# Latent attention between two MLPs: gains in the weights, one token split, a query norm moved into the exponent, a mask as contraction rows, half of the queries turned late

## What is computed

```python
ckr = rms_norm(h, kv_norm) @ w_dkv                    # 256 latents + 32 rotary columns
c_kv = rms_norm(ckr[..., :256], kv_lora_gain)
kv = (c_kv @ w_ukv).reshape(b, s, 16, 64 + 64)        # keys without position, values
k = rope_tail(rms_norm(concat(k_nope, k_rope), k_gain))
q = (rms_norm(rms_norm(h, b_attn_norm) @ w_dq, q_lora_gain) @ w_uq).reshape(b, s, 16, 96)
q = rope_tail(rms_norm(q, q_gain))
mask = key_chunk[None, :] <= (t // 64)[:, None]       # 64 tokens to a chunk
p = softmax(where(mask, q @ k * 96 ** -0.5, -1e30)); out = (p @ v) @ w_o
```

## Time and profile before

| | us |
|---|---|
| median of 3 runs | 1816.54 (1816.24 to 1817.72) |
| the profiled execution, whole | 1816.15 |
| its span in the profile | 1814.3 |
| TensorE busy | 1424.0 (78%) |
| VectorE, ScalarE, GpSimd busy | 550.1, 396.4, 144.9 |
| last matmul of the first MLP to first score of the latent attention | 1485.12 to 1567.00 |
| first score to output product | 1567.00 to 1600.46 |

### The profile page before, as it was taken

How to read it: one execution, slowest core, us unless ns; L and a number is a source line. 1 busy time by engine, 2 the same in 40 slices (tenths; PEclk the granted TensorE clock), 3 DMA queues, 4 the chain that set the end, 5 groups by cost and what they waited for, 6 DMA issues and landing times.

```text
span 1814.3 us, 20829 instructions
## 1 busy us (share of the span) xinstructions
PE 1424.0 (78%) x8548; PEld 856.4 (47%) x8548; DVE 550.1 (30%) x917; ACT 396.4 (22%) x587; POOL 144.9 (8%) x111
## 2 busy tenths in 40 slices
PE   4998978757675667667775767598899978799999
PEld 1884542212221122212221222176799967679997
DVE  1585340000000000000000000167455556635554
ACT  2413310000000000000000000156433344753331
POOL 2660000000000000000000000025200000420000
PEclk8998969787878787787877787789999998999999
DMA  9665539999999999999999999952255543224552
GB/s 378 246 181 223 243 154 422 427 428 428 429 428 429 429 428 428 428 429 429 428 429 428 428 428 429 414 190 89 93 186 186 185 154 99 93 93 143 189 190 105
DMA packets 79490, 542.80 MB, mean 299 GB/s; under 512 B 6370, under 2 KB 9579, under 8 KB 51538
## 3 DMA queue, kind: packets, MB, share of 16 engines
q1 hardware_dynamic: 75728, 535.99, 72.6%
q0 software_dynamic: 2000, 5.77, 1.4%
q10 hardware_dynamic: 1714, 0.36, 0.1%
HBM read 541.01 MB, written 1.08 MB: 299 GB/s over the span
## 4 chain that ended last, share of the span: by engine, by line
DMA 46%; PE 44%; DVE 5%; ACT 3%; issue 2%; POOL 0%; DVEq 0%; SPq 0%; ACTq 0%; POOLq 0%
DMA ring<-in_w_down 22%; DMA ring<-in_w_up 22%; PE bank L1189 10%; PE bank L1190 10%; PE bank L1191 10%; PE bank L1488 3%; PE bank L1505 3%; PE bank L1415 2%; DMA ring<-in_w_in 1%; PE bank L1219 1%; PE bank L1378 1%; PE bank L1359 1%; PE bank L1303 1%; ACT ring_parts L796 1%; DMA ring<-in_w_mod 1%
## 5 line engine op out<-in xcount | busy, mean ns | idle before, releaser
L1488 PE MATMUL bank<-ring,low 128*32 128x512 f32 x2016 | 324.7, 790 | 162.5 <-DMA ring<-in_w_up 137.1
L1488 PEld LDWEIGHTS bank<-ring,low 128*32 128x32 f32 x2016 | 67.7, 133 | 403.2 <-DMA ring<-in_w_up 211.7
L1505 PE MATMUL bank<-ring,low 128*32 128x512 f32 x1008 | 174.1, 828 | 96.0 <-DMA ring<-in_w_down 88.2
L796 ACT ACTIVATE ring_parts<-ring 128x4096 fp32r<-128x4096 f32 (+4 forms) x50 | 163.5, 3277 | 207.7 <-DMA ring<-in_mlp_w_down 94.9
L1781 DVE TENSOR_TENSOR ring_parts<-ring,ring_parts 128x4096 fp32r<-128x4096 f32 (+3 forms) x37 | 154.3, 4174 | 148.2 <-ACT ring_parts L796 148.2
L975 ACT ACTIVATE low<-bank 128x512 f32<-128x512 f32 x16 | 9.6, 597 | 855.8 <-PE bank L1488 855.8
L1189 PE MATMUL bank<-feat_parts,ring_parts 128*128 128x256 f32 x608 | 175.8, 289 | 12.6 <-DVE feat_parts L1845 10.4
L1190 PE MATMUL bank<-feat_parts,ring_parts 128*128 128x256 f32 x640 | 184.1, 288 | 0.0
L1191 PE MATMUL bank<-feat_parts,ring_parts 128*128 128x256 f32 x640 | 183.9, 287 | 0.0
L2107 DVE TENSOR_TENSOR low<-low,bank 128x512 f32<-128x512 f32 x16 | 11.0, 688 | 478.3 <-PE bank L1488 478.3
L1505 PEld LDWEIGHTS bank<-ring,low 128*32 128x32 f32 x1008 | 33.1, 132 | 220.9 <-DMA ring<-in_w_down 142.7
(11 more groups left out here) (345 smaller groups left out, 1968.4 us busy)
## 6 DMA issues: line engine op xcount, KB each, us to landing
ring<-in_w_gate SPq DMA_DIRECT2D x64, 2048.0 KB, 25.7
ring<-in_w_down SPq DMA_DIRECT2D x63, 2048.0 KB, 26.3
ring<-in_w_up SPq DMA_DIRECT2D x62, 2048.0 KB, 23.0
ring<-in_mlp_w_up SPq DMA_DIRECT2D x16, 2048.0 KB, 8.0
ring<-in_mlp_w_down SPq DMA_DIRECT2D x16, 2048.0 KB, 7.9
ring<-in_w_mod SPq DMA_DIRECT2D x12, 2048.0 KB, 11.8
ring<-in_w_in SPq DMA_DIRECT2D x4, 2048.0 KB, 19.1
ring<-in_a_w_in SPq DMA_DIRECT2D x3, 2048.0 KB, 20.1
```

What stands on the lines that cost most here:

```text
L796: last = act.activation(high(n, width)[:, cs], loaded(n, width)[:, cs], ACT.Copy)
L1488: last = pe.matmul((GATE if i < 4 else UP)[32 * j:32 * j + 32, :], xsT[:, k, :], held(n, 2)[:, kk, 512 * j:512 * j + 512], start=(k == 0), ...
L1505: last = pe.matmul(TURN[32 * g:32 * g + 32, :], hidT[:, c, 32 * j:32 * j + 32], held(n, 4)[:, c, 512 * d:512 * d + 512], start=(j == 0 and ...
```

## The change

- **Gains in the weights.** `weights_high` takes a gain and makes eight ScalarE instructions of a chunk, each with its own column of the gain as scale; `gained_low` on VectorE makes the low parts in eight. The inputs have one pair of parts, `hb`, without gain. The query-down split moves between the statistics of the two token tiles, and VectorE does three of its eight low pieces between the last residual and the norm of the second tile.
- **Order.** TensorE: `ckr` (each turned bank as it is ready), `dq` tile 0, turn of the key latents, `dq` tile 1, `ukv` tile 0, turn of the query latents, `ukv` tile 1, `uq`. The splits of the `uq` chunks stand behind the parts of the key latents. Key squares go to ScalarE and are summed by tile.
- **Query norm.** Queries are rotated and turned unscaled. The reciprocal root, one number for each query and head, multiplies the maximum on VectorE and is the scale of the exponential on ScalarE.
- **Mask.** Query and key rows grow from 96 to 98: two rows of ones and of -1e30, brought by two GpSimd DMAs from the constants into rows 96 and 97 of all 16 heads. VectorE's mask add goes. The keys now lie in `feat`, the queries in `low`.
- **Late turn.** The second half of the queries is rotated by VectorE in step 0 of the attention, and turned and copied out in step 1.
- **Output weights.** GpSimd makes both parts of both `wo3` chunks (`split_both`), after the mask transfers.

Context lines of the diff are left out too; the constants table (two rows of ones and -1e30 blocks at its end, the old mask removed), the numbering of splits and the statistics region are not shown.

```diff
...
-hkv, hb = parts(feat_r, 0, KD, T), parts(mid_r, 0, KD, T)
+hb = parts(feat_r, 0, KD, T)
...
+q_squares = [cut(v, 0, NT, HEADS // 2, QK_DIM) for v in (browf, xnf)]
+k_squares = cut(prob, 0, NT, HEADS, QK_NOPE)
+kT3, qT3 = cut(feat, 0, HEADS, T), cut(low, 0, HEADS, T)
+MASKED = QK_DIM + NT
...
-group("dq0", "dq1", chunk=dq_c)
-group("ckvT")
-group(*(f"ukv{t}{n}" for t in range(NT) for n in range(4)), chunk=ukv_c)
-group("dqT0", "dqT1")
+group("dq0", "ckvT")
+group("dq1", chunk=dq_c)
+group(*(f"ukv0{n}" for n in range(4)), "dqT0", "dqT1")
+group(*(f"ukv1{n}" for n in range(4)), chunk=ukv_c)
...
-group(*(f"k3T{i}" for i in range(8)), *(f"q3T{i}" for i in range(8)))
-pair_groups("la")
+group(*(f"k3T{i}" for i in range(4)), *(f"q3T{i}" for i in range(4)), *(f"k3T{i}" for i in range(4, 8)))
+LATE_TURN = 1
+pair_groups("la", {LATE_TURN: [f"q3T{i}" for i in range(4, 8)]})
...
-    pool.wait_ge(sem("q3"), 2)
-    split_low(wo3[0])
-    split_low(wo3[1])
+    def split_both(n):
+        width = width_of(n) // 8
+        full, count = loads(n)
+        pool.wait_ge(full, count)
+        pool.wait_ge(chunk_used, last_user(n, high_slot(n)))
+        for part in range(8):
+            cs = slice(width * part, width * (part + 1))
+            pool.tensor_copy(high(n, 8 * width)[:, cs], loaded(n, 8 * width)[:, cs]).then_inc(sem("w_high_pool"), 1)
+            pool.wait_ge(sem("w_high_pool"), 8 * wo3.index(n) + part + 1)
+            last = pool.tensor_tensor(low_part(n, 8 * width)[:, cs], loaded(n, 8 * width)[:, cs],
+                                      high(n, 8 * width)[:, cs].bitcast(F32), ALU.subtract)
+        last.then_inc(sem("w_low_pool"), 1)
+    for rows, at, after in ((kT3, C_MK, dq_c), (qT3, C_MQ, uq_c[1])):
+        pool.wait_ge(chunk_used, after + 1)
+        pool.dma_start(rows[QK_DIM:MASKED, :, :], I["constants"][0:NT, at:at + T].unsqueeze(1).to_broadcast([NT, HEADS, T]))\
+            .then_inc(sem("ld_mask"), 16)
+    split_both(wo3[0])
+    split_both(wo3[1])
...
-        last = act.activation(high(n, width)[:, cs], loaded(n, width)[:, cs], ACT.Copy)
+        if gain is None:
+            last = act.activation(high(n, width)[:, cs], loaded(n, width)[:, cs], ACT.Copy)
+        else:
+            for k in range(KD):
+                last = act.activation(split_as(n, KD, width // KD)[0][:, k, :], held_as(n, chunks[n])[:, k, :], ACT.Copy,
+                                      scale=vT[:, gain + k:gain + k + 1])
...
-    weights_high(dkv_c)
+    weights_high(dkv_c, gain=V_KV)
...
-    rms("rb", x, xn, D, lambda t: [(sem("xm0"), t + 1)])
-    weights_high(dq_c)
-    for name, dst, v in (("bT", hkv, V_KV), ("bTq", hb, V_B)):
-        for i in range(4):
-            act.wait_ge(*banks.filled(f"bT{i}"))
-            if name == "bTq":
-                act.wait_ge(sem("kv_lo"), i + 1)
-            for k in (2 * i, 2 * i + 1):
-                last = act.activation(dst[0][:, k, :], bk(f"bT{i}")[:, (k % 2) * T:(k % 2 + 1) * T], ACT.Copy,
-                                      scale=vT[:, v + k:v + k + 1])
-            last.then_inc(sem("hi_out"), 1)
+    rms("rb", x, xn, D, lambda t: [(sem("xm0"), t + 1)], [0])
+    weights_high(dq_c, gain=V_B)
+    rms("rb", x, xn, D, lambda t: [(sem("xm0"), t + 1)], [1])
+    parts_high("bT", hb)
...
+    q_junk = cut(prob, 512, NT, Q_LORA)
+    rms("rq", dq, q_junk, Q_LORA, lambda t: [drained(f"dq{t}")], [0])
+    latents_high("ckvT", ckvT, V_KVL, 0, 2)
...
-    latents_high("ckvT", ckvT, V_KVL, 0, 2)
-    rms("rq", dq, cut(prob, 512, NT, Q_LORA), Q_LORA, lambda t: [drained(f"dq{t}")])
+    rms("rq", dq, q_junk, Q_LORA, lambda t: [drained(f"dq{t}")], [1])
+    def key_squares(t):
+        for n in range(4):
+            act.wait_ge(*drained(f"ukv{t}{n}"))
+        act.activation(k_squares[:, t, :, :], kv[:, t, :, 0:QK_NOPE], ACT.Square).then_inc(sem("k_squares"), 1)
+    latents_high("dqT0", dqT, V_QL, 0, 2)
+    latents_high("dqT1", dqT, V_QL, 2, 1)
+    key_squares(0)
...
-    latents_high("dqT0", dqT, V_QL, 0, 2)
-    latents_high("dqT1", dqT, V_QL, 2, 1)
-    head_rms("k3", NT * HEADS, 1.0 / QK_DIM, 1)
-    for half in range(2):
-        if half:
-            act.wait_ge(sem("q3_ss"), half)
-        for t in range(NT):
+    key_squares(1)
+    def query_latents(half, tiles):
+        for t in tiles:
...
-                act.activation(q_squares[:, t, 4 * m:4 * m + 4, :], src, ACT.Square).then_inc(banks.drain_sem(g), 1)
-        head_rms("q3", HEADS, 1.0 / QK_DIM, half + 1)
-        weights_high(wo3[half])
+                act.activation(q_squares[half][:, t, 4 * m:4 * m + 4, :], src, ACT.Square)\
+                    .then_inc(banks.drain_sem(g), 1)
+    query_latents(0, [0])
+    head_rms("k3", NT * HEADS, 1.0 / QK_DIM, 1)
+    query_latents(0, [1])
+    query_latents(1, range(NT))
...
-    heads_out("q3T", qT3, V_QN, range(4))
-    attend_pairs("la", boT)
+    heads_out("k3T", kT3, V_KN, range(4))
+    act.wait_ge(sem("q3_ss"), 2)
+    act.activation(qs[1], qs[0], ACT.Sqrt, bias=eps, scale=1.0 / QK_DIM).then_inc(sem("q3_root"), 1)
+    heads_out("k3T", kT3, V_KN, range(4, 8))
+    def la_between(i):
+        if i == LATE_TURN:
+            heads_out("q3T", qT3, V_QN, (6, 7))
+    def la_scale(i, h):
+        n = HEADS * (i // 8) + head_at(i, h)
+        return qs[2][:, n:n + 1]
+    attend_pairs("la", boT, la_between, la_scale)
...
-    pe.wait_ge(sem("ckv_n"), 1)
-    turn_latents("ckvT", 0, 2, ckr)
-    pe.wait_ge(*drained("ckvT"))
-    need_split(ukv_c)
-    for t in range(NT):
+    def down_product(c, name, width, t, turned=None):
+        need_split(c)
+        token_major_split(f"{name}{t}", hb, split_as(c, KD, width), t * P, width, turned)
+    def keys_values(t):
...
+    down_product(dkv_c, "ckr", KV_LORA + QK_ROPE, 0, "bT")
+    down_product(dkv_c, "ckr", KV_LORA + QK_ROPE, 1)
+    down_product(dq_c, "dq", Q_LORA, 0)
+    pe.wait_ge(sem("ckv_n"), 1)
+    turn_latents("ckvT", 0, 2, ckr)
+    down_product(dq_c, "dq", Q_LORA, 1)
+    pe.wait_ge(*drained("ckvT"))
+    need_split(ukv_c)
+    keys_values(0)
...
+    keys_values(1)
...
+    turn_heads("k3T", K3, (sem("k3"), 1), range(4))
+    turn_heads("q3T", Q3, (sem("q3"), 1), range(4))
+    turn_heads("k3T", K3, (sem("k3"), 1), range(4, 8))
+    pe.wait_ge(sem("ld_mask"), 32)
+    def la_between(i):
+        if i == LATE_TURN:
+            turn_heads("q3T", Q3, (sem("q3"), 2), range(4, 8))
...
+        if t == 0:
+            pe.wait_ge(*drained(f"k3T{i}"))
+            pe.wait_ge(*drained(f"q3T{i}"))
...
-            last = pe.matmul(bk(f"laS{i}")[:, h * n:(h + 1) * n], qT3[0:QK_DIM, hh, t * P:(t + 1) * P],
-                             kT3[0:QK_DIM, hh, 0:n], start=True, stop=True)
+            last = pe.matmul(bk(f"laS{i}")[:, h * n:(h + 1) * n], qT3[0:MASKED, hh, t * P:(t + 1) * P],
+                             kT3[0:MASKED, hh, 0:n], start=True, stop=True)
...
-    pe.wait_ge(*drained("k3T7"))
-    pe.wait_ge(*drained("q3T3"))
-    pe.wait_ge(*drained("q3T7"))
-    attend_pairs("la", la_scores, la_values, bo, ident)
+    attend_pairs("la", la_scores, la_values, bo, ident, la_between)
...
-            add_biases(i, s)
-            dve.tensor_reduce(at_m[:, i % 4, :], s, AX, ALU.max, negate=True).then_inc(sem(pre + "_max"), 1)
+            if add_biases:
+                add_biases(i, s)
+            last = dve.tensor_reduce(at_m[:, i % 4, :], s, AX, ALU.max, negate=True)
+            if scales:
+                link(last)
+                last = dve.tensor_tensor(at_m[:, i % 4, :], at_m[:, i % 4, :], scales(i), ALU.mult)
+            last.then_inc(sem(pre + "_max"), 1)
...
+    def gained_low(n, gain, ks):
+        if ks[0] == 0:
+            dve.wait_ge(sem("w_high"), high_no(n) + 1)
+        w, hi, lo = held_as(n, chunks[n]), *split_as(n, KD, width_of(n) // KD)
+        for k in ks:
+            last = dve.scalar_tensor_tensor(out=lo[:, k, :], in0=w[:, k, :], scalar=vT[:, gain + k:gain + k + 1],
+                                            in1=hi[:, k, :].bitcast(F32), op0=ALU.mult, op1=ALU.subtract)
+        if ks[-1] == KD - 1:
+            last.then_inc(sem("w_low"), 1)
...
+                if t == 1:
+                    gained_low(dq_c, V_B, range(0, 3))
...
-    weights_low(dq_c)
-    for name, dst, v in (("bT", hkv, V_KV), ("bTq", hb, V_B)):
-        for i in range(4):
-            dve.wait_ge(*hi_out(f"{name}{i}"))
-            for k in (2 * i, 2 * i + 1):
-                last = lo_part(dst, k, bk(f"bT{i}")[:, (k % 2) * T:(k % 2 + 1) * T], v)
-            last.then_inc(sem("kv_lo") if name == "bT" else banks.drain_sem(f"bT{i}"), 1)
+    parts_low("bT", hb)
+    gained_low(dq_c, V_B, range(3, KD))
...
-    def latents_out(name, dst, width):
...
-    latents_out("dq", dq, Q_LORA)
-    weights_low(uq_c[0])
+    latents_out("dq", dq, Q_LORA, [0])
+    dve.wait_ge(*drained("dq0"))
+    normed("rq", dq, dq, Q_LORA, 0)
...
-    for t in range(NT):
-        dve.wait_ge(*drained(f"dq{t}"))
-    for t in range(NT):
```

(73 more changed lines are left out.)

67 lines of the change are left out of this document (34 added, 33 removed).

## The result

The changed kernel takes 1796.89 us (median of 4 runs, 1795.36 to 1801.24) against 1816.39 (1812.87 to 1817.72) of the kernel before in the same session: a ratio of 0.9899, with a 95% interval of 0.9876 to 0.9923. It is faster by 19.5 us, about 1%. The forecast was 26.5 us and 1790.0, its range 1785 to 1799: sign and range held, the size was 7 us off.

A forecast was written before the change was run, and what follows sets the result against it. Between the two MLPs, a chain of hand-overs with three TensorE gaps was taken to bound the kernel. Terms -26.9 (earlier first exponential), -1.0 (mask), +1.0 (late turn) and 0.4 (hand-overs) gave -26.5: 1790.0 us, range 1785 to 1799.

The forecast's parts named there:

- schedule of stage A: From the first MLP's last matmul to the attention's first exponential: reordering puts that exponential at 1541.7 instead of 1568.65, -26.9 us.
- Key-value product: Down product before the attention: 48 matmuls, partly at slow clock, taken as 9.0 us with ends 6.6 and 13.1.
- Turns: Just before the attention: 48 of the 64 turns stand ahead of it, 5.8 us, rounded to 6.0.
- gap two: TensorE's 4.35 us wait before 1518.24: ScalarE sits 4.27 us at the first up-query weights, needed latents queued behind.
- relief of ScalarE from the output splits: Before the attention: two output-weight splits of 3.60 us each stood ahead of ScalarE's key copies; GpSimd makes them, hidden.
- Mask transfer: Before the first score: 32 KB from GpSimd's queue lands in 3.9 us, costing nothing; at 7.4, some 0.5 us.
- Mask in the contraction: In the attention: sixteen adds of 0.42 us go, dependent products of 0.2 us each come instead, -1.0 us.
- rival (d): Output product: GpSimd copies from 3.2 us on delay the second chunk; at 4 us 1829.7, slower than before; chance 0.02.
- rival (c): Output weights: GpSimd's copy is slower than its two-input operation; at twice 1.27 us, 18.6 us late, 1808.6; chance 0.09.
- +1.0 for the late turn: Attention steps 0 to 3: the second rotation, turns and copies moved there cost 1.0 us, with ends 0 and 3.7.
- own sign of being wrong: Attention steps 0 to 3: their sum longer than before by more than 2 us would show the forecast wrong.
- rival (b): Start of the attention: the clock falls again, steps 0 to 3 run at half clock, 1793.6 us; chance 0.09.

The follow-up runs named there:

- up-query edit: The kernel before, with only the split of the first up-query weights moved behind the parts of the turned key latents: 1811.38 us.
- GpSimd late: The changed kernel, but GpSimd waits for the ninth maximum of the latent attention before it splits the output weights: 1800.02 us.
- combined kernel: The changed kernel with the query factor as scalar operand, mask rows by SyncE, and GpSimd's output split after the second rotation: 1791.19 us, ratio to before 0.9884.
- filled gaps: The changed kernel with three added matmuls of unused result where TensorE waits for the mask rows and the second rotation: 1799.13 us.
- spread turn: The combined kernel with the late turn spread over steps 0 to 3, one bank in each: 1793.78 us, ratio to before 0.9878.

## Why the prediction was right in sign and off in size

**The schedule of stage A: right.** I had the first exponential 56.6 us after the first MLP's end, it came after 56.34. First down product: +6.3 said, +6.11 measured. Key-value product: 9.0 us said, 7.55 measured (1496.02 to the issue of the up-query weights at 1503.57); I had expected more of it at half clock than before, and the clock was full from 1498.0 on, 2 us after its start, where before it was 0.72 from 1499 to 1501. End of the query down product: +24.3 said, +23.4. Value product, each half: 5.45 said, 5.5. End of the up-query product: +48.6 said, +47.5 (the turns begin at 1537.43). Turns: 6.0 said, 5.40. The split of the query weights in eight took 4.15 instead of 3.4, hidden. The up-query edit alone gave 3.68 in the kernel before, so gap two was what I took it for. The relief of ScalarE from the output splits was not free, as the same move made the kernel before slower; that it pays in the changed kernel because the scaling of the queries is gone and GpSimd's start comes late is argued, no run separates it.

**Mask transfer: off in size, in the list of bounds.** I took the landing of 3.9 us; it was 6.8, near the upper end of 7.4. ScalarE then waited 0.98 for the first maximum, and the run with the rows on SyncE's queue won 0.63 of it back. The gains in A covered it.

**Mask in the contraction: -1.0 said, little measured.** Stage C has seven of the sixteen adds fewer and is 0.3 longer (19.93 against 19.64). TensorE sets the pace there (18.6 of 19.9 us). Where neither GpSimd nor the clock disturbed, in steps 4 to 7 of the run with GpSimd late, four steps took 6.81 against 7.16 before: 0.35 won. The scale product is 0.16 alone, near my 0.2. I had called the reduction of 0.42 the nearest row, but VectorE's reciprocal of 128x2 was nearer in kind, and it would have given the right size:

```profile
L1970 DVE RECIPROCAL st<-st 128x2 f32<-128x2 f32 x16 | 2.5, 155 | 0.0
```

Two sums there are loose. "16 x 0.2 = 3.4" should be 16 times the 0.22 that an add costs more, 3.5. In rival (d) the wait of GpSimd on itself, which (c) counts, is left out.

**The step that failed: steps 0 to 7 of the attention,** where I had +1.0 for the late turn and nothing else. They cost 7.95, 7.5 of it in steps 0 to 3, where my own sign of being wrong stood at 2. The rest of the gap of 7.6 between the 26.5 forecast and the 18.94 that A to D gained is mostly the mask's 1.0 that did not come. Three things in it:
- *The late turn's own order*: 3.2 us (15.69 against 12.50, both at full clock and with no VectorE instruction of B stretched), where I wrote +1.0. I had counted its 16 turns as saved in A and as lying beside other work in B; TensorE works through them one after the other in both places. The end of my own range, 3.7, was the nearer one.
- *VectorE behind GpSimd*: 2.9 us (20.12 against 17.21). My rival (c) had the contention, and even the condition of two SBUF inputs, but priced it only on GpSimd's side, as a late delivery. GpSimd was done at 1570.1, 31.6 us after its start and 16 us before need, at the lower end of what I had (1565 to 1578 from 1534.4, so 30.6 to 43.6). The victim was VectorE, whose rotation stood ahead of the late turn. The 1.274 of the earlier trace rows, which I read as evidence against contention, is the length of GpSimd's instructions and says nothing of VectorE's.
- *The clock*: 1.5 us (17.21 against 15.69), on top of what contention adds. The two runs differ in more than the clock. In steps 0 to 3, where it was 0.69 and 1.00, they took 10.40 and 8.54; in steps 4 to 7, at full clock in both, the combined kernel took 0.3 longer, with GpSimd at work and the pair of 0.33 in place of the 0.16. So the clock's own part is nearer 1.9. That is rival (b), at 0.09: its sign, a clock below 1 from about 1546 on, showed in the profile. My reason against it, that the gaps before each earlier fall were over 4 us, did not hold: the waits before this fall were 1.89 and 0.58. Its price of 3.6 was of the right size where nothing else held the steps up: the kernel before with its output split on GpSimd lost 4.6 by it.

These three and 0.3 that no run explains (12.50 against 12.17) make up the 7.95, but only in this order of taking them away. In steps 0 to 3 contention and clock overlap: with the clock full and contention left (filled gaps, whose added products lay in TensorE's waits) they took 12.51, with contention gone and the clock at 0.69 10.40, with both gone 8.54. So the clock alone was worth nothing there, contention alone 2.1, both 4.0.

That the time lay inside the range owes something to luck: the range had 2.7 for a worse late turn and rival (b), but no term for VectorE behind GpSimd.

The Trainium skill (SBUF — State Buffer, Who interferes with whom) says that VectorE and GpSimd share one pair of ports as an exclusive lock, that a VectorE instruction with two SBUF inputs contends with a GpSimd instruction that reads SBUF, and, of the modes in which VectorE takes both pairs, that the first to issue holds it for the whole instruction and the other is fully blocked. The trace agrees to 0.03 us: the products end when GpSimd's subtractions end. Had I used that rule, the price per VectorE instruction would have been up to 1.27 us, and I would have looked for the short ones on the chain.

**Open.** What makes the clock fall: after, at 1546, it fell near the same pattern of waits through which the combined kernel kept full speed; the spread turn, whose TensorE was busy 0.89 and 0.91 us in the two slices where the combined one had 0.89 and 0.96, lost it. These are the slices, first of the spread turn, then of the combined kernel (again); in both TensorE had waited 2.15 us for the first exponential, and its work up to there was the same:

```profile
1537.65:1539.65 2.00, 0.89 (x8) 0.70 (x7) 1.82 (x8) 1.97 (x4) 0.00 (x0) 1.00 0.85 320
1539.65:1541.65 2.00, 0.91 (x3) 0.52 (x4) 1.93 (x4) 2.00 (x9) 0.21 (x1) 0.67 0.00 0
...
1543.25:1545.25 2.00, 0.89 (x8) 0.70 (x7) 1.82 (x8) 1.97 (x3) 0.00 (x0) 1.00 0.90 335
1545.25:1547.25 2.00, 0.96 (x7) 0.78 (x8) 1.93 (x4) 2.00 (x9) 0.21 (x1) 1.00 0.00 1
```

Filling the waits only moved the fall. What decides between two kernels that are equal up to that point I can't say.

## What to carry to other kernels

Work that is moved to GpSimd to relieve another engine is paid for by VectorE: each of its instructions with two SBUF inputs may stand until GpSimd's current one ends. So start GpSimd behind VectorE's critical section, and write small dependent products with a scalar operand instead of a second tensor. Cutting GpSimd's work into shorter instructions should shorten each wait, but no run here tries it. And a step that is moved into a later loop on a busy engine is not hidden by moving it: count its time on that engine in both places, and test it undone (here the late turn was worth nothing: 113.0 us from A to D with it, 112.75 without). Last, two losses can hide behind each other: that a change of one alone gives nothing back does not show that it costs nothing.

## What the runs showed of the hardware that was not expected

- A product of 128x2 took 0.16 us alone and up to 1.14 beside GpSimd; as two products of 128x1 with a scalar operand, 0.33 to 0.34 for the pair, beside GpSimd or not. A rotation of 2.2 us became 4.5. GpSimd can be the loser too: its subtraction of 1.27 took 3.21 beside VectorE's key scaling.
- The exponential of 128x128 took 0.37 us with the constant scale of the kernel before (the row below) and 0.46 (the row at 1546.25 above) with a column of the query factor as scale: 0.09 more for each of 32. The Trainium skill (ScalarE: Activation LUTs, What ACT_TABLE_LOAD costs) has about 93 ns for each such operand; the trace agrees. No run here separates what it cost.
- A transfer of 32 KB from GpSimd's queue, two partitions of 16 KB each, took 6.4 and 6.8 us from issue to landing. By SyncE's queue the same rows were there when TensorE came, at most 5.1 us after their issue (1537.11 to 1542.16).
- GpSimd's conversion of 512 columns took 0.61 us, close to the memset's 0.52 in the earlier trace rows; with the subtraction and its wait 1.90 for each part.

ScalarE's first exponential in the kernel before:

```profile
1568.65 0.37 ACT L885 ACTIVATE brow<-bank,st 128x128 f32<-128x128 f32 x1 [1.86 <-DVE st L1966]
```
